# Four of eight weight splits of a pair of heads placed behind the head's chain, sticks and probabilities

## The chip, the cores and the metric

The kernel runs on one core of a Trainium2 chip. The metric is device time in microseconds of one launch; the median over the runs is compared. The engines are TensorE (PE), VectorE (DVE), ScalarE (ACT), GpSimd (POOL) and SyncE (SP), which issues the loads. Each runs its own instructions in order and waits on semaphores.

## The reference

One layer of an encoder with 544 tokens (512 of a prompt, 32 of running streams with 256 cached frames), width 1024, in float32. The part in which the change lies is the combined input projection and the stick-breaking attention of eight heads:

```python
xn = rms_norm(x, g_mix)
h = xn @ w_in              # u | q | k | v | gates
z = jnp.einsum('bqhd,bkhd->bhqk', q, k) * (SB_HEAD_DIM ** -0.5)
causal = k_pos[None, :] < q_pos[:, None]
log_not = jnp.where(causal, jax.nn.log_sigmoid(-z), 0.0)
suffix = lax.cumsum(log_not, axis=3, reverse=True) - log_not
a = jnp.where(causal, jnp.exp(jax.nn.log_sigmoid(z) + suffix), 0.0)
o = jnp.einsum('bhqk,bkhd->bqhd', a, v)
...
merged = gate_a * (y_pool @ w_pool_up) + gate_b * (y_sb @ w_sb_up)
x = x + merged @ w_out
```

Behind it come an MLP and a gated embedding, which the change doesn't touch.

## The kernel before

Each float32 operand is split into a high part (rounded to the type that TensorE takes) and a low part (the rest), and a product is three matmuls: high by high, low by high, high by low. A weight tile is 128 x 1024, made of eight 128 x 128 blocks, and gives a result of 128 x 544 with 48 matmuls.

The stage runs over four pairs of heads; pairs 1 and 2 are a hardware loop, pairs 0 and 3 are written out. A pair has eight weight tiles: 0 to 3 are q, k, v and the pooling input u, 4 to 7 are gates. TensorE's order in pairs 1 and 2 is: tiles 0 and 1, `sums` of head 1 of the pair before, tile 2, its `outputs`, `scores` of head 0, tile 3, `v_rows`, tiles 4 and 5, `sums(0)`, tile 6, `outputs(0)`, `scores(1)`, tile 7. In pair 0 tiles 0 to 3 come ahead of the scores.

**Splits.** `split(t)` stands on two engines. ACT waits until the tile has been loaded to `raw` and a slot of the ring of four split tiles is free, and writes the high part (L853); DVE waits for ACT and writes the low part, raw less high (L1820). The loads (L651, on SP's queue) go to a ring of two buffers: the load of tile t waits until DVE has split tile t - 2, since both share a buffer. Splits run three tiles ahead (`AHEAD`): `split(AHEAD + j)` of pair i is for the tile 3 + j of the pair, so j = 2 and 3 are its tiles 5 and 6, and j = 6 and 7 are tiles 1 and 2 of the next pair. Counted on from the pair's own tiles these are called tiles 9 and 10 below, and the one from j = 5 is tile 8.

**The head's chain.** After `scores`, ACT takes Abs, Exp and Ln of 128 x 1280 (`chain`, L929 to L933); DVE makes the stick, max(z, 0) plus that (`stick`, L1906); GpSimd masks four diagonal blocks (L767); ACT copies the high part (`stick_hi`, L938); DVE adds later blocks (`stick_later`, L1913 to L1916), whose high part ACT takes (L940); DVE takes both low parts (`stick_lo`, L1921 and L1923). TensorE's `sums` need them. Then ACT takes the exponential (`prob`, L946), GpSimd masks it, ACT writes its high part (`prob_hi`, L951), DVE its low part (`prob_lo`, L1927), and `outputs` (L1428, L1430) multiply by V. The parts of stick and of probabilities lie at the same place in `b_hi` and `b_lo`; stick and probabilities share `work`.

**GpSimd** does, beside the masks, the window sums of the pooling mixer (L747), its means (L757 to L760), and issues copies and accumulating copies of weights in HBM (L782, L789) after each head's probabilities, for a later stage. These share the DMA engines with the loads.

The order of each engine is that of the code, written by hand; no scheduler moves anything. What the change moves stands in `pair` of ACT and `pair` of DVE.

Of the kernel before, what the change touches and what calls it, by code (L numbers as in the profile page):

```python
# [32 lines left out]
S1_PER = 8  # L33
# [13 lines left out]
AHEAD = W_RING - 1  # L47
# [250 lines left out]
def hybrid_step_kernel(nc, w_tiles, x_t, p_t, ck_t, cv, state_t, w_grp, vecs,  # L298
# [5 lines left out]
    with ctx:  # L304
# [118 lines left out]
        def rows_of(hh):  # L423
            return slice(DH * hh, DH * hh + DH)
# [416 lines left out]
        def _(act):  # L841
            act.dma_start(vec[:, :], vecs).then_inc(vec_in, 16)

            def split(t, i=0, per=0, left=None):
                if left is None:
                    left = results_by(t - W_RING)

                s = t % W_RING

                act.wait_ge(raw_in[t % RAW_RING], 16 * (t // RAW_RING + t % RAW_RING) + i * (16 * per // RAW_RING))  # L850
                if left is not None:
                    act.wait_ge(full, left + i * per)
                act.activation(w_hi[:, s, :, :].rearrange("p k c -> p (k c)"), raw[:, t % RAW_RING, :],  # L853
                               ACT.Copy).then_inc(whi_done, 1)
# [93 lines left out]
            def prob_hi(hh, i):  # L948
                g = 2 * i + hh
                act.wait_ge(pm_done, g * QB + QB)  # L950
                act.activation(b_hi[:, SOF:SOF + Z_COLS], work[:, :], ACT.Copy).then_inc(phi_done, 1)  # L951
# [16 lines left out]
            def pair(i):  # L968
                first = isinstance(i, int) and i == 0
                last = isinstance(i, int) and i == PAIRS - 1  # L970
                if not first:
                    split(AHEAD + 0, i, S1_PER, 0)
                act.wait_ge(taken, 1 + i * S1_PER)
                for hh in range(2):
                    r = rows_of(hh)
                    act.activation(b_hi[r, QOF + hh * SEQ:QOF + (hh + 1) * SEQ], ev[r, 0, 0:SEQ], ACT.Copy)\
                       .then_inc(qkhi_done, 1)
                if not first:
                    split(AHEAD + 1, i, S1_PER, 1)
                act.wait_ge(taken, 2 + i * S1_PER)  # L980
                for hh in range(2):
                    r = rows_of(hh)
                    act.activation(b_lo[r, KOF + hh * SEQ:KOF + (hh + 1) * SEQ], ev[r, 1, 0:SEQ], ACT.Copy)\
                       .then_inc(qkhi_done, 1)
                act.dma_start(k_t[i, :, :], ev[:, 1, 0:TOK]).then_inc(kv_out[0], 16)
                if first:
                    split(AHEAD + 1)
                if not first:
                    prob(1, i - 1)
                split(AHEAD + 2, i, S1_PER, 2)  # L990
                if not first:
                    prob_hi(1, i - 1)
                chain(0, i)
                split(AHEAD + 3, i, S1_PER, 3)
                stick_hi(0, i)
                act.wait_ge(taken, 3 + i * S1_PER)
                act.dma_start(v_t[i, :, :], ev[:, 2, 0:TOK]).then_inc(kv_out[1], 16)
                act.wait_ge(vt_done, i + 1)
                act.activation(v_parts[:, :, V_HI, :], o_heads, ACT.Copy).then_inc(vhi_done, 1)
                split(AHEAD + 4, i, S1_PER, 4)  # L1000
                if last:

                    tables(SIGMOID)
                    for m in range(KT):
                        sigmoid(m)
                    tables(LOG_EXP)
                    mean_hi(0)
                    mean_hi(1)
                split(AHEAD + 5, i, S1_PER, 5)
                prob(0, i)  # L1010
                split(AHEAD + 6, i, S1_PER, 6)
                prob_hi(0, i)
                if last:
                    group_hi(0)
                    group_hi(1)

                    act.wait_ge(z_done, HEADS)
                    mean_hi(2)
                    mean_hi(3)
                chain(1, i)  # L1020
                split(AHEAD + 7, i, S1_PER, 7)
                if last:
                    group_hi(2)
                    group_hi(3)
                stick_hi(1, i)

            pair(0)
            with act.Fori(1, PAIRS - 1) as i:
# [778 lines left out]
        def _(dve):  # L1807
# [189 lines left out]
            def pair(i):  # L1997
                first = isinstance(i, int) and i == 0
                last = isinstance(i, int) and i == PAIRS - 1
                q, k, v = (ev[:, n, 0:TOK] for n in range(3))  # L2000
                if not first:
                    split(AHEAD + 0, i, S1_PER)

                dve.wait_ge(full, 1 + i * S1_PER)
                dve.scalar_tensor_tensor(out=halves(q), in0=pair_result(0, i), scalar=DH ** -0.5, in1=halves(rn[:, :]),
                                         op0=ALU.mult, op1=ALU.mult).then_inc(taken, 1)
                if first:
                    normed(1, k, i, S1_PER, pair_result(1, i)).then_inc(taken, 1)
                    normed(2, v, i, S1_PER, pair_result(2, i)).then_inc(taken, 1)
                    dve.wait_ge(taken, 3)  # L2010
                if first:
                    q_parts(i)
                    k_parts(i)
                    pool_input(i)
                    split(AHEAD + 1)
                    running_q(i)
                    dve.tensor_copy(kst[:, i, :], k[:, SEQ:TOK])
                    dve.tensor_copy(vst[:, i, :], v[:, SEQ:TOK])
                    split(AHEAD + 2)
                else:  # L2020
                    running_q(i)
                    q_parts(i)
                    split(AHEAD + 1, i, S1_PER)
                    dve.wait_ge(kv_out[0], 16 * i)
                    normed(1, k, i, S1_PER, pair_result(1, i)).then_inc(taken, 1)
                    dve.wait_ge(taken, 2 + i * S1_PER)
                    dve.tensor_copy(kst[:, i, :], k[:, SEQ:TOK])
                    k_parts(i)
                    split(AHEAD + 2, i, S1_PER)
                    prob_lo(1, i - 1)  # L2030
                    dve.wait_ge(kv_out[1], 16 * i)
                    normed(2, v, i, S1_PER, pair_result(2, i)).then_inc(taken, 1)
                    dve.wait_ge(taken, 3 + i * S1_PER)
                    dve.tensor_copy(vst[:, i, :], v[:, SEQ:TOK])
                if not first:
                    head_out(1, i - 1)
                    stick(0, i)
                    split(AHEAD + 3, i, S1_PER)
                    stick_later(0, i)

                if not first:
                    pool_input(i)
                if first:
                    stick(0, i)
                    split(AHEAD + 3)
                    stick_later(0, i)
                stick_lo(0, i)
                dve.wait_ge(vhi_done, i + 1)
                dve.tensor_tensor(v_parts[:, :, V_LO, :], o_heads, v_parts[:, :, V_HI, :], ALU.subtract)\
                   .then_inc(vlo_done, 1)  # L2050
                split(AHEAD + 4, i, S1_PER)
                gate(0, i)
                split(AHEAD + 5, i, S1_PER)
                if last:

                    dve.wait_ge(mean_done, GROUPS)
                gate(1, i)
                split(AHEAD + 6, i, S1_PER)
                if last:
                    mean_lo(0)  # L2060
                    mean_lo(1)
                prob_lo(0, i)
                gate(2, i)
                if last:
                    group_lo(0)
                head_out(0, i)
                if last:
                    group_lo(1)
                    mean_lo(2)
                    mean_lo(3)  # L2070
                    gate(3, i)
                else:
                    split(AHEAD + 7, i, S1_PER)
                stick(1, i)
                if last:
                    group_lo(2)
                    group_lo(3)
                    stick_later(1, i)
                    split(AHEAD + 7, i, S1_PER)
                    stick_lo(1, i)  # L2080
                    for s in kv_out:
                        dve.wait_ge(s, 16 * PAIRS)
                else:
                    gate(3, i)
                    stick_later(1, i)
                    stick_lo(1, i)

            pair(0)
            with dve.Fori(1, PAIRS - 1) as i:
# [472 lines left out]
```

## Time and profile before

| | us |
|---|---|
| runs (three), median | 772.29 (772.29 to 773.46) |
| profiled execution, its own time | 773.24 |
| its span from first to last instruction | 771.5 |
| TensorE busy | 754.4 (98%) |
| DVE busy | 556.8 (72%) |
| ACT busy | 421.9 (55%) |
| GpSimd busy | 147.6 (19%) |
| the pairs of heads | about 34 to 245 of the span |

The mean granted clock of TensorE is 0.995. The busy shares are over the whole program; within the pairs the engines' order and the idle times before each instruction, with what ended them, are in the timelines. A row of a timeline gives the start, the duration, the engine and line, the operation, the tiles written and read, and in brackets the idle time before it and who ended it.

### The profile page before, as it was taken

The page shows a single profiled execution, that of the slowest core. Times are in us where ns is not written, and L with a number is a line of the kernel's source. Part 1 is how long each engine was busy: PE and PEld are TensorE (multiplying, and loading weights), DVE is VectorE, ACT ScalarE, POOL GpSimd, SP SyncE. Part 2 cuts the span into 40 slices and gives each one's busy share as a digit, 9 for nine tenths or more (in the row PEclk, how much of TensorE's full clock was granted, in tenths as well). Part 3 has the DMA queues.
Part 4 walks back from the last instruction along what each step waited for, and adds up shares of the span by engine and source line. Part 5 has one row for each costly group of instructions (what it writes and reads, how often), then busy time and mean ns, then how long its engine had stood idle before and what let it go on. Part 6 is the DMA issues. An engine that isn't in the chain of part 4 may idle for free.

```text
span 771.5 us, 14459 instructions
## 1 busy us (share of the span) xinstructions
PE 754.4 (98%) x5902; PEld 745.6 (97%) x5902; DVE 556.8 (72%) x705; ACT 421.9 (55%) x524; POOL 147.6 (19%) x259
## 2 busy tenths in 40 slices
PE   8999999999999999999999999999999999999994
PEld 8999999999999999999999999999999999999993
DVE  6776556566567527499999669965998567677986
ACT  7545535435485442377674357634763356556575
POOL 1051342453471332001111112111101000000001
PEclk9999999999999999999999999999999999999997
DMA  7254848769769899936797999999887857342503
GB/s 241 91 190 133 233 149 221 228 195 260 221 173 263 264 246 300 256 112 216 215 342 202 370 251 340 250 322 318 236 268 210 281 165 222 107 115 74 198 1 116
DMA packets 49516, 165.78 MB, mean 215 GB/s; under 512 B 6320, under 2 KB 8368, under 8 KB 49456
## 3 DMA queue, kind: packets, MB, share of 16 engines
q0 software_dynamic: 18688, 67.18, 35.2%
q1 hardware_dynamic: 28512, 94.16, 34.9%
q10 hardware_dynamic: 2256, 3.60, 1.3%
q8 instruction: 43, 0.70, 0.3%
q14 instruction: 17, 0.14, 0.1%
HBM read 160.39 MB, written 71.63 MB: 301 GB/s over the span
## 4 chain that ended last, share of the span: by engine, by line
PE 90%; DVE 5%; ACT 3%; issue 1%; DMA 1%; SPq 0%; POOL 0%; POOLq 0%; DVEq 0%
PE psum L1654 23%; PE psum L1705 16%; PE psum L1353 15%; PE psum L1359 14%; PE psum L1356 14%; PE psum L1402 1%; PE psum L1430 1%; DMA raw<-w_tiles 1%; PE psum L1428 1%; PE psum L1390 1%; PE psum L1389 1%; ACT xt L1273 1%; PE psum L1409 1%; PE psum L1414 1%; ACT L887 0%
## 5 line engine op out<-in xcount | busy, mean ns | idle before, releaser
L861 ACT ACTIVATE w_hi<-raw_more 128x1024 fp32r<-128x1024 f32 x83 | 87.7, 1056 | 72.2 <-PE psum L1705 43.3
L1353 PE MATMUL psum<-a_hi,w_hi 128*128 128x272 f32 x576 | 120.5, 290 | 1.4 <-DVE w_lo L1870 1.0
L1828 DVE TENSOR_TENSOR w_lo<-raw_more,w_hi 128x1024 fp32r<-128x1024 f32 x83 | 101.1, 1222 | 25.9 <-ACT w_hi L861 25.5
L1359 PE MATMUL psum<-a_hi,w_lo 128*128 128x272 f32 x576 | 119.2, 288 | 0.0
L1356 PE MATMUL psum<-a_lo,w_hi 128*128 128x272 f32 x576 | 118.8, 288 | 0.0
L1654 PE MATMUL psum<-u_hi,w_hi 128*128 128x272 f32 x560 | 116.3, 289 | 1.5 <-ACT h_of L1105 1.0
L1654 PE MATMUL psum<-u_hi,w_lo 128*128 128x272 f32 x560 | 115.7, 288 | 0.0
L1654 PE MATMUL psum<-u_lo,w_hi 128*128 128x272 f32 x560 | 115.5, 287 | 0.0
L1353 PEld LDWEIGHTS psum<-a_hi,w_hi 128*128 128x128 f32 x576 | 90.3, 188 | 2.0 <-DVE w_lo L1870 1.2
L1356 PEld LDWEIGHTS psum<-a_lo,w_hi 128*128 128x128 f32 x576 | 90.5, 189 | 0.0
L1654 PEld LDWEIGHTS psum<-u_hi,w_hi 128*128 128x128 f32 x560 | 87.9, 188 | 2.4 <-issue 1.9
L1359 PEld LDWEIGHTS psum<-a_hi,w_lo 128*128 128x128 f32 x576 | 89.9, 189 | 0.0
L1654 PEld LDWEIGHTS psum<-u_lo,w_hi 128*128 128x128 f32 x560 | 88.4, 189 | 0.0
L1654 PEld LDWEIGHTS psum<-u_hi,w_lo 128*128 128x128 f32 x560 | 87.4, 188 | 0.0
L1820 DVE TENSOR_TENSOR w_lo<-raw,w_hi 128x1024 fp32r<-128x1024 f32 x41 | 51.2, 1248 | 43.3 <-ACT w_hi L853 43.1
L1828 DVE TENSOR_TENSOR w_lo<-raw,w_hi 128x1024 fp32r<-128x1024 f32 x44 | 53.6, 1222 | 20.6 <-ACT w_hi L861 12.3
L789 POOL DMA_DIRECT2D sums_t<-sums_t x32 | 27.5, 1011 | 192.2 <-PE psum L1654 101.7
L1356 PE MATMUL psum<-b_lo,w_hi 128*128 128x272 f32 x304 | 62.8, 288 | 0.0
L782 POOL DMA_DIRECT2D sums_t<-w_tiles x64 | 33.6, 536 | 150.9 <-DMA sums_t<-w_tiles 51.2
L861 ACT ACTIVATE w_hi<-raw 128x1024 fp32r<-128x1024 f32 x39 | 41.2, 1056 | 36.0 <-PE psum L1705 21.7
L853 ACT ACTIVATE w_hi<-raw 128x1024 fp32r<-128x1024 f32 x46 | 48.1, 1050 | 22.0 <-DMA raw<-w_tiles 13.2
L1353 PE MATMUL psum<-b_hi,w_hi 128*128 128x272 f32 x288 | 60.0, 289 | 0.0
(287 smaller groups left out, 1562.7 us busy)
## 6 DMA issues: line engine op xcount, KB each, us to landing
sums_t<-w_tiles POOLq DMA_DIRECT2D x96, 512.0 KB, 8.1
raw<-w_tiles SPq DMA_DIRECT2D x63, 512.0 KB, 4.4
raw_more<-sums_t SPq DMA_DIRECT2D x42, 512.0 KB, 6.7
raw_more<-w_tiles SPq DMA_DIRECT2D x41, 512.0 KB, 5.1
sums_t<-sums_t POOLq DMA_DIRECT2D x32, 512.0 KB, 10.9
raw<-sums_t SPq DMA_DIRECT2D x22, 512.0 KB, 5.0
xt<-x_t SPq DMA_DIRECT2D x8, 272.0 KB, 5.8
y_t<-xt SPq DMA_DIRECT2D x16, 136.0 KB, 1.9
```

The costliest lines, as they stand in the source:

```text
L782: pool.dma_start(sum_tile(i, what), sum_tile(i, of)).then_inc(sums_in, 16)
L789: pool.dma_start(sum_tile(i, what), sum_tile(i, of), accum_op=ALU.add).then_inc(sums_in, 16)
L853: act.activation(w_hi[:, s, :, :].rearrange("p k c -> p (k c)"), raw[:, t % RAW_RING, :], ACT.Copy).then_inc(whi_done, 1)
L861: act.activation(w_hi[:, t % W_RING, :, :].rearrange("p k c -> p (k c)"), src, ACT.Copy)\
L1273: act.activation(x, x, ACT.Copy, scale=g_fin[:, m:m + 1]).then_inc(xg_last, 1)
L1353: pe.matmul(base[:, h, :], w_hi[:, s, wk, :], at(hi, k, h * HALF, (h + 1) * HALF), start=(opens and q == 0), stop=False, skip_group_check= ...
L1356: pe.matmul(base[:, h, :], w_hi[:, s, wk, :], at(lo, k, h * HALF, (h + 1) * HALF), start=False, stop=False, skip_group_check=True)
L1359: mm = pe.matmul(base[:, h, :], w_lo[:, s, wk, :], at(hi, k, h * HALF, (h + 1) * HALF), start=False, stop=(closes and q == len(ks) - 1), s ...
L1654: mm = pe.matmul(out[:, two, :], w_part[:, t % W_RING, 2 * k + two, :], u_part[:, op, k, :], start=(OPENS[s] and k == 0 and w_part is w_hi ...
L1705: mm = pe.matmul(out[:, two, :], w_part[:, t % W_RING, 2 * k + two, :], h_part[:, i * HALF:(i + 1) * HALF], start=(OPENS[s] and k == 0 and ...
L1820: dve.tensor_tensor(w_lo[:, s, :, :].rearrange("p k c -> p (k c)"), raw[:, t % RAW_RING, :], w_hi[:, s, :, :].rearrange("p k c -> p (k c)" ...
L1828: dve.tensor_tensor(w_lo[:, t % W_RING, :, :].rearrange("p k c -> p (k c)"), src, w_hi[:, t % W_RING, :, :].rearrange("p k c -> p (k c)"), ...
```

## The change

In each pair four splits are placed later, on both engines. On ACT: tile 5 behind `prob_hi` of the head before (it stood between `prob` and `prob_hi`), tile 6 behind `stick_hi(0)` (between `chain` and `stick_hi`), tile 9 behind `prob_hi(0)`, tile 10 behind `stick_hi(1)`. On DVE: tile 5 behind `prob_lo`, tile 6 from between `stick` and `stick_later` to behind `stick_lo`, tile 9 behind `prob_lo(0)`, tile 10 from ahead of `stick(1)` to behind `stick_lo(1)`. In pair 0 there is no head before, so tile 5 stays. TensorE's, GpSimd's and SP's programs are the same.

```diff
--- ACT, pair(i)
-                split(AHEAD + 2, i, S1_PER, 2)
+
                 if not first:
                     prob_hi(1, i - 1)
+                split(AHEAD + 2, i, S1_PER, 2)
                 chain(0, i)
+                stick_hi(0, i)
                 split(AHEAD + 3, i, S1_PER, 3)
-                stick_hi(0, i)
...
                 prob(0, i)
+                prob_hi(0, i)
                 split(AHEAD + 6, i, S1_PER, 6)
-                prob_hi(0, i)
...
                 chain(1, i)
-                split(AHEAD + 7, i, S1_PER, 7)
                 if last:
                     group_hi(2)
                     group_hi(3)
                 stick_hi(1, i)
+                split(AHEAD + 7, i, S1_PER, 7)
--- DVE, pair(i)
                     k_parts(i)
+                    prob_lo(1, i - 1)
                     split(AHEAD + 2, i, S1_PER)
-                    prob_lo(1, i - 1)
...
                     stick(0, i)
-                    split(AHEAD + 3, i, S1_PER)
                     stick_later(0, i)
...
                 if first:
                     stick(0, i)
-                    split(AHEAD + 3)
                     stick_later(0, i)
                 stick_lo(0, i)
+                split(AHEAD + 3, i, S1_PER)
...
-                split(AHEAD + 6, i, S1_PER)
                 if last:
                     mean_lo(0)
                     mean_lo(1)
                 prob_lo(0, i)
+                split(AHEAD + 6, i, S1_PER)
...
-                else:
-                    split(AHEAD + 7, i, S1_PER)
                 stick(1, i)
                 if last:
...
                     stick_later(1, i)
+                    stick_lo(1, i)
                     split(AHEAD + 7, i, S1_PER)
-                    stick_lo(1, i)
...
                     stick_later(1, i)
                     stick_lo(1, i)
+                    split(AHEAD + 7, i, S1_PER)
```

ACT in pair 0, from the end of head 0's chain (`work`) over the stick's high parts (`b_hi`, `later_hi`), V's (`b_hi` from `psum`) and the exponential, before:

```order
L933 ACTIVATE work<-work 128x1280
L853 ACTIVATE w_hi<-raw 128x1024
L938 ACTIVATE b_hi<-work 128x1280
L940 ACTIVATE later_hi<-later 128x384
L997 DMA v_t<-ev 128x544
L999 ACTIVATE b_hi<-psum 128x4x2x64
L853 ACTIVATE w_hi<-raw 128x1024 x2
L946 ACTIVATE work<-psum 128x1280
L853 ACTIVATE w_hi<-raw 128x1024
L951 ACTIVATE b_hi<-work 128x1280
```

The same place after (lines further down count one more):

```order
L933 ACTIVATE work<-work 128x1280
L938 ACTIVATE b_hi<-work 128x1280
L940 ACTIVATE later_hi<-later 128x384
L853 ACTIVATE w_hi<-raw 128x1024
L998 DMA v_t<-ev 128x544
L1000 ACTIVATE b_hi<-psum 128x4x2x64
L853 ACTIVATE w_hi<-raw 128x1024 x2
L946 ACTIVATE work<-psum 128x1280
L951 ACTIVATE b_hi<-work 128x1280
L853 ACTIVATE w_hi<-raw 128x1024
```

The first L853 (tile 6) moved past the stick's two high parts, the last (tile 9) past the probabilities'; the pair between them (tiles 7 and 8) stays in its place.

DVE at the same place, from the stick (`work`) to the low part of V (L2049), before:

```order
L1906 SCALAR_TENSOR_TENSOR work<-psum,work 128x1280
L1820 TENSOR_TENSOR w_lo<-raw,w_hi 128x1024
L1913 TENSOR_TENSOR later<-work 128x128
L1914 TENSOR_TENSOR later<-work 128x128
L1916 TENSOR_TENSOR later<-work,later 128x128
L1921 TENSOR_TENSOR b_lo<-work,b_hi 128x1280
L1923 TENSOR_TENSOR later_lo<-later,later_hi 128x384
L2049 TENSOR_TENSOR b_hi<-psum,b_hi 128x4x128
```

and after:

```order
L1907 SCALAR_TENSOR_TENSOR work<-psum,work 128x1280
L1914 TENSOR_TENSOR later<-work 128x128
L1915 TENSOR_TENSOR later<-work 128x128
L1917 TENSOR_TENSOR later<-work,later 128x128
L1922 TENSOR_TENSOR b_lo<-work,b_hi 128x1280
L1924 TENSOR_TENSOR later_lo<-later,later_hi 128x384
L1821 TENSOR_TENSOR w_lo<-raw,w_hi 128x1024
L2049 TENSOR_TENSOR b_hi<-psum,b_hi 128x4x128
```

The split of tile 6 moved from ahead of the three later sums to behind the two low parts, ahead of V's low part (L2049).

## Rows read from the trace of the kernel before

**Rows 1.** The page's first part: busy us, share of the span, instructions.

```profile
PE 754.4 (98%) x5902; PEld 745.6 (97%) x5902; DVE 556.8 (72%) x705; ACT 421.9 (55%) x524; POOL 147.6 (19%) x259
```

**Rows 2.** Busy time by stretch: length, engines, clock, DMA share, GB/s.

```profile
34.00:94.40 60.40, 59.93 (x464) 58.96 (x463) 41.02 (x55) 31.77 (x31) 18.32 (x33) 1.00 0.56 178
94.40:152.80 58.40, 58.40 (x458) 57.88 (x457) 35.33 (x48) 26.91 (x27) 21.90 (x39) 1.00 0.69 199
...
128.00:132.00 4.00, 4.00 (x35) 4.00 (x33) 3.85 (x6) 1.57 (x3) 0.00 (x0) 1.00 0.48 149
```

**Rows 3.** TensorE's waits, 34 to 262 us: total, times, longest.

```profile
PE psum L1353 <- issue: 1.1, 1, 1.1
```

**Rows 4.** Timeline of TensorE: start, us, instruction, idle time before and releaser.

```profile
50.55 0.46 PE L1353 MATMUL psum<-a_hi,w_hi 128*128 128x272 f32 x2
...
56.63 0.50 PE L1428 MATMUL psum<-b_hi 128*128 128x512 f32 x1
...
115.18 0.39 PE L1428 MATMUL psum<-b_hi 128*128 128x512 f32 x1
```

**Rows 5.** Timeline of DVE, pairs 0 to 2.

```profile
38.95 1.49 DVE L1906 SCALAR_TENSOR_TENSOR work<-psum,work 128x1280 f32<-128x1280 f32 x1 [1.25 <-ACT work L933]
40.74 1.23 DVE L1820 TENSOR_TENSOR w_lo<-raw,w_hi 128x1024 fp32r<-128x1024 f32 x1 [0.30 <-ACT w_hi L853]
...
44.02 1.26 DVE L1916 TENSOR_TENSOR later<-work,later 128x128 f32<-128x128 f32 x1
45.20 1.48 DVE L1921 TENSOR_TENSOR b_lo<-work,b_hi 128x1280 fp32r<-128x1280 f32 x1
46.60 0.55 DVE L1923 TENSOR_TENSOR later_lo<-later,later_hi 128x384 fp32r<-128x384 f32 x1
...
54.67 1.91 DVE L1927 TENSOR_TENSOR b_lo<-work,b_hi 128x1280 fp32r<-128x1280 f32 x1
...
100.95 1.55 DVE L1820 TENSOR_TENSOR w_lo<-raw,w_hi 128x1024 fp32r<-128x1024 f32 x1
...
113.06 1.49 DVE L1927 TENSOR_TENSOR b_lo<-work,b_hi 128x1280 fp32r<-128x1280 f32 x1 [0.27 <-ACT b_hi L951]
...
122.70 1.23 DVE L1820 TENSOR_TENSOR w_lo<-raw,w_hi 128x1024 fp32r<-128x1024 f32 x1 [4.59 <-ACT w_hi L853]
...
135.96 0.72 DVE L1865 TENSOR_TENSOR ev<-psum,rn 128x544 f32<-128x544 f32 x1 [0.19 <-PE psum L1359]
```

**Rows 6.** Timeline of ACT, pairs 0 to 2.

```profile
46.22 2.00 ACT L853 ACTIVATE w_hi<-raw 128x1024 fp32r<-128x1024 f32 x2
50.75 1.24 ACT L946 ACTIVATE work<-psum 128x1280 f32<-128x1280 f32 x1 [2.53 <-PE psum L1402]
...
53.37 1.26 ACT L951 ACTIVATE b_hi<-work 128x1280 fp32r<-128x1280 f32 x1
...
111.75 1.27 ACT L951 ACTIVATE b_hi<-work 128x1280 fp32r<-128x1280 f32 x1 [0.26 <-POOL work L767]
...
132.84 1.06 ACT L853 ACTIVATE w_hi<-raw 128x1024 fp32r<-128x1024 f32 x1
...
138.31 1.24 ACT L946 ACTIVATE work<-psum 128x1280 f32<-128x1280 f32 x1 [0.31 <-PE psum L1402]
```

**Rows 7.** Timeline of GpSimd (POOL), pair 0.

```profile
40.51 2.11 POOL L767 TENSOR_SCALAR_AFFINE_SELECT work<-work 128x128 f32<-128x128 f32 x4 [36.44 <-DVE work L1906]
...
52.12 1.04 POOL L767 TENSOR_SCALAR_AFFINE_SELECT work<-work 128x128 f32<-128x128 f32 x4 [7.00 <-ACT work L946]
...
55.23 2.84 POOL L757 TENSOR_SCALAR gates<-gates 128x557 f32<-128x557 f32 x1
```

**Rows 8.** Loads issued near 42, 113 and 124: KB, us to landing.

```profile
raw<-w_tiles SPq DMA_DIRECT2D x1, 512.0 KB, 3.5
...
raw<-w_tiles SPq DMA_DIRECT2D x1, 512.0 KB, 9.7
...
raw<-w_tiles SPq DMA_DIRECT2D x1, 512.0 KB, 7.4
```

## The prediction

> **What bounds the kernel now.** I read the page's busy shares first: TensorE is busy for 754.4 of the 771.5 us [rows 1]. Then the busy time by stretch: the whole change lies in the four pairs of heads, from 34 to 245 us. In the pairs' first stretch TensorE is busy for 59.93 of 60.40 us and in the next for 58.40 of 58.40, at the full clock (1.00, the 2.4 GHz level) [rows 2]. The reader should see that there is nothing to win there but 0.47 us of idle time, which lies before tile 4 of pair 0, ahead of every edit, and 1.1 us at the end of the last pair, where TensorE begins the pooled tiles [rows 3]. So the ceiling of any gain is about 1.6 us, and the question is whether the change puts a new wait on TensorE. Its program is the same before and after; what changes is when the operands arrive. For that I read the timelines of DVE, ACT and GpSimd around pair 0 and pair 1 and looked for the smallest margin between an operand's end and the matmul that needs it. It is in pair 0: the low half of head 0's probabilities ends at 54.67 + 1.91 = 56.58 [rows 5] and the product with V starts at 56.63 [rows 4]. In pair 1 the same step ends at 113.06 + 1.49 = 114.55 and is needed at 115.18: 0.63 us of margin [rows 4, 5]. Pair 0 is tight because its tile 3 is done before the scores, so one tile of 6.1 us fewer (50.55 to 56.63 is tile 6) stands between scores and sums.
>
> **The splits of tiles 5 and 9 (behind the high half of the probabilities; numbers by the pair's own count).** In pair 1 ACT's high half starts at 111.75 after 0.26 us of idle time that the masks on GpSimd ended [rows 6]: the split ran inside the wait for the masks, so moving it frees nothing there. DVE's low half started 0.27 us after its split [same pair, rows 5], again on ACT's end. The split itself comes 1.3 us (ACT) and about 2.9 us (DVE: 1.49 for the low half that is now first, 1.3 for the later start) later, and with it the next load of its buffer. Cost 0: behind either place TensorE still has two tiles of 6.1 us or more to do before it needs them. Pair 0 has no such step for tile 5.
>
> **The split of tile 6 (behind stick).** In pairs 1 to 3 the gain is in GpSimd: four masks took 2.11 us with a split on DVE beside them (40.51, split at 40.74) and 1.04 without (52.12) [rows 5, 7]. The stick chain comes 1 us earlier, and that is off the path. The Trainium skill says why (SBUF — State Buffer, Who interferes with whom): a VectorE instruction with two SBUF inputs contends with a GpSimd instruction that reads SBUF. These rows agree.
>
> The split then ends, in pair 1, about where the next one does now (100.95 + 1.55 = 102.5 [rows 5]) or sooner, and tile 6 starts near 109.1 (115.18 less a tile): no wait. In pair 0, step by step:
> - Stick ends at 38.95 + 1.49 = 40.44, the masks at 40.51 + 1.04 = 41.55 instead of 42.62: 1.07 earlier.
> - The three later sums end at 45.28 now (44.02 + 1.26), so at 44.2. From there to the end of the two low halves it is 1.95 us now (45.20 to 46.60 + 0.55): 46.15.
> - ACT does the split after the sums' high half: 44.25 + 0.5 + 1.06 = 45.8. DVE does it after the low halves: 46.15 + 1.2 = 47.35, instead of 40.74 + 1.23 = 41.97. Tile 6 starts at 50.55: 3.2 us of margin, no wait of TensorE.
> - But the raw ring has two buffers, so tile 8's load waits for this split. It was issued near 42 and landed after 3.5 us [rows 8], ahead of its place on ACT (the second of the two splits from 46.22, near 47.2 [rows 6]). Now it is issued at 47.4 and lands at 50.9. ACT stands in that wait with the probabilities behind it: split 50.95 to 52.0, exponential from 51.9 instead of 50.75: 1.15 late.
> - Exponential 1.24, masks 1.04, high half: it can start at 54.25 instead of 53.37 (0.88 late, since the split of tile 9 no longer stands before it). High half 1.28, so the low half starts on DVE at 55.55 and takes 1.49 (row of pair 1) to 1.91 (row of this place): 57.05 to 57.45.
> - TensorE, which came for it at 56.63, waits 0.4 to 0.8 us. I take 0.7, nearer to the row of this place.
>
> The same page says that whichever of the two starts first holds the pair of ports for its whole instruction, and the other blocks. The low half would start at 55.55, ahead of GpSimd's scaling (55.23 now, and about 1 us later then), and so run in 1.49: 0.4 us of wait, 772.7 in all. The row of now speaks against it: 1.91 at 54.67, though it began 0.56 us before the scaling [rows 5, 7].
>
> Bounds of this term: if DVE's later sums get ahead of GpSimd's window sums (the last of them, 128 x 128, takes 1.26 us here, as long as a split of 128 x 1024 [rows 5], so it is held up), tile 8's load comes 1 us sooner and the wait is 0; if the load took 9.7 us, the worst of the pairs' loads [rows 8], it is 7 us. That worst row was issued among the copies of sums, with the DMA engines full; 47 us is ahead of the first copies, which follow the masks of 52.12, so I take 3.5.
>
> **The split of tile 10 (behind stick of head 1).** DVE's stick no longer waits for the split, so head 1's chain comes about 2 us sooner; TensorE has tile 0 and tile 1 of the next pair before it needs it. The split's end moves by 4.9 us in pair 1, from 122.70 + 1.23 = 123.9 [rows 5] to about 128.8 (after ACT's two steps of stick and DVE's two low halves), and with it the load of the tile that ACT splits at 132.84 [rows 6]. That load took 7.4 us when issued at 124 [rows 8], among copies; at 128 to 132 the DMA engines are 0.48 busy [rows 2], so I take 4 us: landed at 132.8, no cost. The last pair's 1.1 us hangs on gate and group work that isn't moved: unchanged.
>
> **Sum.** 0 + 0.7 + 0 on the profiled execution's 773.24 gives 773.9. That execution is 0.95 above the median of the runs shown, 772.29; against that median it is 773.0, which I forecast.
>
> **Rivals.**
> 1. No wait at all (the lower bound above): 772.3. For it: the 1.07 us that the masks give back, and each of the chain's estimates is only 0.3 us wide. Against: the zero margin at 56.58.
> 2. Faster: the earlier chains close some idle time of TensorE. At most 1.6 us of it is in the stretch, and I find no edit that reaches either piece; 771 at best.
> 3. Slower, by one mechanism: the load behind the split of tile 10 stays among the copies. If it takes 7.4 us again, it lands at 136.3; ACT 1.06 and DVE 1.23 make 138.6, and the new keys (behind that split on DVE, due at 135.96 [rows 5]) follow at 138.7, 2.7 late; ACT converts them ahead of head 1's probabilities, whose exponential starts at 138.31 [rows 6] after 0.3 us of idle time. Less that and about 0.6 us of margin at the product with V, TensorE waits some 1.8 us, in pairs 1 to 2 and 2 to 3 each: 773.0 + 3.6 = 776.6, or 774.8 if only one pair. It decides from a landing time of about 5.5 us. For it: in this stretch loads take 7.4 to 9.7. Against: the copies are nearly done by 128.
> 4. The change does what it says but the load of tile 8 is slower still, by 1 us: 774.0; it belongs to the forecast's own range.
>
> **How the numbers follow.** Forecast (a wait of 0.3 to 1.5 us in pair 0): 0.48. No wait: 0.29. Slower by late loads: 0.19. Faster: 0.04. A measurement of this kernel can tell about 0.2%, 1.5 us, from no change. Forecast and rival 1 lie within it, less a few hundredths where small waits add up: same 0.76, slower 0.21, faster 0.03. The likeliest case alone spans 772.5 to 773.9; the range takes in no wait, with the runs' own spread below it, and one late load: 771.9 to 775.0.
>
> **What would show it.** In the profile after: masks of head 0 near 1.04 us in every pair; tile 8's split on ACT waiting for a DMA until about 51 us; the exponential of pair 0 near 51.9; a wait of 0.4 to 0.8 us before the product with V near 57, named to DVE's b_lo; and no wait of TensorE in pairs 1 and 2. I am wrong if that wait is missing, if TensorE waits for w_lo anywhere in the pairs, or if ACT waits for raw in pairs 2 and 3 so long that the probabilities slip.

## The result, and the profile after

The changed kernel takes 773.52 us (median of 14 runs, 772.83 to 775.28), the kernel before 772.64 in the runs beside it (14 runs, 772.15 to 773.54). The ratio is 1.0015, with a 95% interval of 1.0008 to 1.0022: about 0.15% slower, below the 0.2% that the prediction named as the least that can be told, though the interval leaves 1 out. The forecast was 773.0, the range 771.9 to 775.0. The profiled execution took 773.29 us, its span 771.5 us at a clock of 0.995, as before.

The sum line of the page hardly moves (answers to [rows 1]):

```profile
PE 754.7 (98%) x5902; PEld 745.6 (97%) x5902; DVE 559.5 (73%) x705; ACT 421.7 (55%) x524; POOL 145.2 (19%) x259
```

The busy time by stretch (length, then busy time and instructions of PE, PEld, DVE, ACT, POOL, then clock, DMA share, GB/s; answers to [rows 2]) says in which pair something happened:

```profile
34.00:94.40 60.40, 59.32 (x460) 58.22 (x459) 39.94 (x54) 30.60 (x30) 16.45 (x33) 1.00 0.55 172
94.40:152.80 58.40, 58.40 (x458) 57.88 (x458) 36.12 (x47) 26.92 (x27) 20.98 (x39) 1.00 0.73 198
152.80:211.30 58.50, 58.48 (x457) 57.74 (x456) 36.37 (x47) 26.80 (x27) 23.67 (x40) 1.00 0.84 222
```

TensorE has 0.61 us less in pair 0's stretch than before; the next two are as full as they were, but for 0.02 us in the last (58.50 of 58.50 before). To place it, I lined up the 5902 matmuls of the two traces one by one and looked where the difference of their start times steps. It is -0.44 us before the first edit (the start of a run varies: the kernel before, profiled again, began the pairs 0.15 earlier), and then steps four times: +0.75 at pair 0's product with V, +0.29 at the product of pair 2's head 1 (203 us), +0.21 in the last pair (234 us), and -0.77 at 362 us, far behind the change. At the end it is +0.05: the earlier start hides most of the cost in these two traces.

**Pair 0.** Timeline of TensorE after (start, us, instruction, idle time before and releaser; answers to [rows 4]):

```profile
56.94 0.50 PE L1429 MATMUL psum<-b_hi 128*128 128x512 f32 x1 [0.60 <-DVE b_lo L1928]
...
115.49 0.39 PE L1429 MATMUL psum<-b_hi 128*128 128x512 f32 x1
```

The wait is there in pair 0 and not in pair 1. Its origin is on ACT (answers to [rows 6]; L853 is a split, L946 the exponential, L951 the probabilities' high half):

```profile
44.24 1.04 ACT L853 ACTIVATE w_hi<-raw 128x1024 fp32r<-128x1024 f32 x1
...
45.67 1.05 ACT L853 ACTIVATE w_hi<-raw 128x1024 fp32r<-128x1024 f32 x1
50.61 1.06 ACT L853 ACTIVATE w_hi<-raw 128x1024 fp32r<-128x1024 f32 x1 [3.89 <-DMA raw<-w_tiles]
51.58 1.22 ACT L946 ACTIVATE work<-psum 128x1280 f32<-128x1280 f32 x1
54.00 1.27 ACT L951 ACTIVATE b_hi<-work 128x1280 fp32r<-128x1280 f32 x1 [1.21 <-POOL work L767]
```

The row at 50.61 is the one to see: tile 8's split stands 3.89 us for its load, and the exponential follows it without a gap. That load went out once DVE had done tile 6's split (45.57 + 1.21, below) and landed after 3.6 us:

```profile
raw<-w_tiles SPq DMA_DIRECT2D x1, 512.0 KB, 3.6
```

DVE in the same stretch (answers to [rows 5]), then GpSimd (answers to [rows 7]):

```profile
42.51 1.26 DVE L1917 TENSOR_TENSOR later<-work,later 128x128 f32<-128x128 f32 x1
...
45.57 1.21 DVE L1821 TENSOR_TENSOR w_lo<-raw,w_hi 128x1024 fp32r<-128x1024 f32 x1
...
55.31 1.58 DVE L1928 TENSOR_TENSOR b_lo<-work,b_hi 128x1280 fp32r<-128x1280 f32 x1 [1.74 <-ACT b_hi L951]
```

```profile
40.07 1.04 POOL L767 TENSOR_SCALAR_AFFINE_SELECT work<-work 128x128 f32<-128x128 f32 x4 [36.00 <-DVE work L1907]
...
56.04 2.34 POOL L757 TENSOR_SCALAR gates<-gates 128x557 f32<-128x557 f32 x1
```

The masks take 1.04 us instead of 2.11, and the later sums end 1.5 us earlier (0.44 of it the start); the exponential is still 0.83 later (1.27 with the start taken off), because it now queues behind a load.

**Between pairs 2 and 3.** The two weight loads issued between 186.5 and 189 us took 5.9 us, and one of them is the tile that ACT splits at 193.59. The loads, and the timelines of ACT, DVE and TensorE after:

```profile
raw<-w_tiles SPq DMA_DIRECT2D x2, 512.0 KB, 5.9
```

```profile
193.59 1.06 ACT L853 ACTIVATE w_hi<-raw 128x1024 fp32r<-128x1024 f32 x1 [2.85 <-DMA raw<-w_tiles]
...
197.88 1.24 ACT L946 ACTIVATE work<-psum 128x1280 f32<-128x1280 f32 x1
...
201.56 1.49 DVE L1928 TENSOR_TENSOR b_lo<-work,b_hi 128x1280 fp32r<-128x1280 f32 x1 [2.85 <-ACT b_hi L951]
...
203.11 0.50 PE L1429 MATMUL psum<-b_hi 128*128 128x512 f32 x1
```

The same place before: no wait for the load, the exponential 1.1 us earlier (0.8 with pair 0's lag taken off). The first matmul's row is 0.50 us long after and 0.40 before: the lost time stands inside a busy share, and only the start times show it.

```profile
191.28 1.06 ACT L853 ACTIVATE w_hi<-raw 128x1024 fp32r<-128x1024 f32 x1
...
196.75 1.24 ACT L946 ACTIVATE work<-psum 128x1280 f32<-128x1280 f32 x1 [0.24 <-PE psum L1402]
...
202.61 0.40 PE L1428 MATMUL psum<-b_hi 128*128 128x512 f32 x1
```

**The last pair.** TensorE's step is at 234.79, at the first matmul behind the product with V. It starts 0.05 us behind the end of the DVE row that takes a gate's result out of `psum`, where TensorE writes its results (`gates<-psum`, 234.02 + 0.72), and tile 9's split now stands between the low half and that row. After:

```profile
231.48 1.49 DVE L1928 TENSOR_TENSOR b_lo<-work,b_hi 128x1280 fp32r<-128x1280 f32 x1 [1.30 <-ACT b_hi L951]
232.89 1.22 DVE L1821 TENSOR_TENSOR w_lo<-raw,w_hi 128x1024 fp32r<-128x1024 f32 x1
234.02 0.72 DVE L1942 TENSOR_TENSOR gates<-psum,rn 128x544 f32<-128x544 f32 x1
...
234.79 0.39 PE L1335 MATMUL psum<-b_lo,b_hi 128*128 128x272 f32 x1
```

Before, that row ended at 233.07, 0.96 us ahead of its matmul. In the six traces with tile 9 late in the last pair (this one, numbers 1, 3, 6, 11 and 12) the matmul starts 0.05 to 0.06 us behind the row's end; in the other eight the row ends 0.96 to 0.97 us ahead of it. DVE couldn't start the low half sooner to make up for it: with the split out of the way, its mean_lo comes a split earlier and runs beside the masks of the probabilities, which take twice as long (after, then before):

```profile
228.10 2.04 POOL L767 TENSOR_SCALAR_AFFINE_SELECT work<-work 128x128 f32<-128x128 f32 x4 [2.48 <-ACT work L946]
...
228.49 0.70 DVE L1988 TENSOR_TENSOR mean_lo<-upad,mean_hi 128x512 fp32r<-128x512 f32 x1
...
230.17 1.27 ACT L951 ACTIVATE b_hi<-work 128x1280 fp32r<-128x1280 f32 x1 [2.14 <-POOL work L767]
```

```profile
227.49 1.03 POOL L767 TENSOR_SCALAR_AFFINE_SELECT work<-work 128x128 f32<-128x128 f32 x4 [2.42 <-ACT work L946]
...
228.56 1.28 ACT L951 ACTIVATE b_hi<-work 128x1280 fp32r<-128x1280 f32 x1 [0.19 <-POOL work L767]
```

So the low half starts at 231.48, against 230.95 before, which is about TensorE's own lag of 0.61, though the split no longer stands ahead of it. Which of the two, the split's place or the longer masks, would be enough by itself was not tried.

**At 362 us** TensorE meets ACT's evictions (L1105, one line lower after). Before, then after:

```profile
361.44 0.60 ACT L1105 ACTIVATE h_of<-psum 128x544 f32<-128x544 f32 x1
...
362.15 0.48 PE L1654 MATMUL psum<-u_hi,w_hi 128*128 128x272 f32 x2 [0.53 <-issue]
```

```profile
361.36 0.60 ACT L1106 ACTIVATE h_of<-psum 128x544 f32<-128x544 f32 x1
...
362.29 0.42 PE L1655 MATMUL psum<-u_hi,w_hi 128*128 128x272 f32 x2
```

The profile names no releaser for the 0.53 us. But in all fourteen traces of this study that matmul starts, within 0.02 us, at the later of two times: 0.12 us behind the matmul before it, or 0.10 us behind the end of that eviction (before: 361.33 + 0.12 against 362.05 + 0.10; after: 362.17 + 0.12 against 361.96 + 0.10). ACT's chain was 0.09 us earlier after, TensorE 0.84 later; so 0.77 us of what TensorE lost upstream (0.70 at this matmul, the rest at the next) was lost where it would have waited anyway. The longest wait of ACT's chain ahead of it is for a weight load among GpSimd's copies (its split at 325.94 waited 7.15 us before, the one at 329.42 4.53 us after). What sets these landings in one execution was not tried.

### The profile page after: what moved, and what is told of

It reads as the page before. It is cut to its first block, busy times and chain, and to the rows that moved or that the text cites. A ratio compares the mean times of both kernels' runs of the same rounds, so it can differ in the third digit from the quotient of the medians.

```text
span 771.5 us, 14459 instructions
## 1 busy us (share of the span) xinstructions
PE 754.7 (98%) x5902; PEld 745.6 (97%) x5902; DVE 559.5 (73%) x705; ACT 421.7 (55%) x524; POOL 145.2 (19%) x259
## 4 chain that ended last, share of the span: by engine, by line
PE 85%; issue 6%; DVE 4%; ACT 3%; POOL 1%; DMA 0%; POOLq 0%; SPq 0%; DVEq 0%
PE psum L1655 23%; PE psum L1706 16%; PE psum L1354 13%; PE psum L1360 13%; PE psum L1357 13%; PE psum L1403 1%; PE psum L1429 1%; PE psum L1431 1%; PE psum L1391 1%; PE psum L1390 1%; ACT xt L1274 1%; ACT L887 0%; DMA raw<-w_tiles 0%; PE psum L1410 0%; DVE w_lo L1829 0%
## 5 line engine op out<-in xcount | busy, mean ns | idle before, releaser
L1821 DVE TENSOR_TENSOR w_lo<-raw,w_hi 128x1024 fp32r<-128x1024 f32 x41 | 54.5, 1338 | 20.5 <-ACT w_hi L853 20.4
L1829 DVE TENSOR_TENSOR w_lo<-raw,w_hi 128x1024 fp32r<-128x1024 f32 x44 | 53.6, 1222 | 19.4 <-ACT w_hi L861 12.3
L853 ACT ACTIVATE w_hi<-raw 128x1024 fp32r<-128x1024 f32 x46 | 47.9, 1049 | 33.9 <-DMA raw<-w_tiles 27.1
```

The source lines that it names most:

```text
L1821: dve.tensor_tensor(w_lo[:, s, :, :].rearrange("p k c -> p (k c)"), raw[:, t % RAW_RING, :], w_hi[:, s, :, :].rearrange("p k c -> p (k c)" ...
L1829: dve.tensor_tensor(w_lo[:, t % W_RING, :, :].rearrange("p k c -> p (k c)"), src, w_hi[:, t % W_RING, :, :].rearrange("p k c -> p (k c)"), ...
```

## The experiments

All ratios are against the kernel before on the same chip in the same job, with 95% intervals. "Step" is a step of the difference of matmul starts against the trace of the kernel before, counted over all the matmuls over which it grows.

**1. Pair 0's tile 6 back in its place** (all else as changed):

```diff
+                if first:
+                    split(AHEAD + 3, i, S1_PER, 3)
                 stick_hi(0, i)
-                split(AHEAD + 3, i, S1_PER, 3)
+                if not first:
+                    split(AHEAD + 3, i, S1_PER, 3)
```

(the same on DVE).

> The changed kernel with tile 6's split in pair 0 alone back in its old place on both engines. Theory (the late split holds up the load of tile 8, and ACT stands in that wait with the exponential behind it): TensorE's 0.60 us of idle time before pair 0's product with V is gone, its program runs 0.75 us earlier from there on, and the two smaller steps in pair 3 (0.29 and 0.16 us) stay; time about 0.4 to 0.5 us over the kernel before, ratio near 1.0006. Rival (DVE and GpSimd get in each other's way at the low half of the probabilities, whatever the load does): at least 0.4 us of that wait stays. Second rival (the loss is in pairs 1 to 3): time as the changed kernel, ratio near 1.0015.

Measured: 772.63 against 772.71, ratio 1.0001 [0.9992, 1.0010]. No wait and a step of -0.13 at pair 0's product (its first matmul takes 0.40 us, that of the kernel before 0.50 [rows 4], so that kernel loses a little there too), +0.42 at 203, +0.21 at 234, -0.57 at 362.

```profile
49.95 1.24 ACT L946 ACTIVATE work<-psum 128x1280 f32<-128x1280 f32 x1 [2.62 <-PE psum L1406]
...
55.82 0.40 PE L1432 MATMUL psum<-b_hi 128*128 128x512 f32 x1
```

With one split in one pair put back, no difference is left that can be measured.

**2. Only pair 0's tile 6 late** (the kernel before with that one edit):

```diff
-                split(AHEAD + 3, i, S1_PER, 3)
+                if not first:
+                    split(AHEAD + 3, i, S1_PER, 3)
                 stick_hi(0, i)
+                if first:
+                    split(AHEAD + 3, i, S1_PER, 3)
```

> The kernel before with tile 6's split of pair 0 alone placed late on both engines. Theory: the wait of 0.6 us before pair 0's product with V is there, and no other new one; TensorE is 0.75 us later from there; ratio near 1.0008 to 1.0010. Second rival (the loss is in pairs 1 to 3): no wait, ratio 1.0000.

Measured: 773.40 against 772.71, ratio 1.0010 [1.0001, 1.0019]. One step of +1.13 at pair 0's product, none else in the pairs, -0.46 at 362: +0.66 from start to end, and +0.69 by the medians.

```profile
51.00 1.06 ACT L853 ACTIVATE w_hi<-raw 128x1024 fp32r<-128x1024 f32 x1 [3.90 <-DMA raw<-w_tiles]
51.97 1.22 ACT L946 ACTIVATE work<-psum 128x1280 f32<-128x1280 f32 x1
...
57.72 0.50 PE L1431 MATMUL psum<-b_hi 128*128 128x512 f32 x1 [1.00 <-DVE b_lo L1930]
```

The edit makes the cost by itself. The step is larger than in the changed kernel, mainly because the low half takes 1.92 us, not 1.58; tile 9's split still stands ahead of it here (see the last section).

**3. Keep tile 6 late, take tile 8's split from ahead of the exponential** (the changed kernel; in pair 0 tile 8's split behind both halves; ACT's side):

```diff
-                split(AHEAD + 5, i, S1_PER, 5)
+                if not first:
+                    split(AHEAD + 5, i, S1_PER, 5)
                 prob(0, i)
                 prob_hi(0, i)
+                if first:
+                    split(AHEAD + 5, i, S1_PER, 5)
```

> The changed kernel with tile 8's split in pair 0 also moved, behind the high and low half of the probabilities; tile 6's split stays late, so the load of tile 8 lands as late as in the changed kernel (near 50.6). Theory (the late load costs time only because ACT waits for it ahead of the exponential): the exponential starts when the sums end, about 1.2 us sooner than in the changed kernel, and the 0.60 us wait before the product with V is gone; the steps of pair 3 stay; ratio near 1.0006. Rival (contention on DVE and GpSimd): the wait stays at 0.4 us or more.

Measured: 772.42 against 772.71, ratio 0.9994 [0.9985, 1.0003]. Pair 0 has no wait, and the -0.13 of number 1; the load is as late, but nothing that matters stands behind it:

```profile
50.66 1.24 ACT L946 ACTIVATE work<-psum 128x1280 f32<-128x1280 f32 x1 [3.60 <-PE psum L1406]
...
56.52 0.40 PE L1432 MATMUL psum<-b_hi 128*128 128x512 f32 x1
```

So it is the place of the wait in ACT's order, not the late split or the late load, that costs.

**4. The kernel before again**, as a control.

> The kernel before, unchanged, as a control. Every theory: ratio 1.0000 within the interval. Its trace tells whether two differences between the traces of before and after belong to the change: TensorE's start, 0.44 us earlier after, which lies ahead of every edit, and an idle time of 0.53 us at 362 us that stood in before alone. If either differs between two runs of this same kernel, it belongs to the run and not to the change.

Measured: 772.91, ratio 1.0000 [0.9991, 1.0009]. Steps: -0.15 at the start, +0.06 at pair 0's product and no other in the pairs, -0.14 at 362, where the wait is 0.39 us.

**5. Only tile 10 late; 6. only tiles 5 and 9 late** (the kernel before with these edits of the change alone; ACT's side of 5, then of 6):

```diff
-                split(AHEAD + 7, i, S1_PER, 7)
                 if last:
                     group_hi(2)
                     group_hi(3)
                 stick_hi(1, i)
+                split(AHEAD + 7, i, S1_PER, 7)
```

```diff
-                split(AHEAD + 2, i, S1_PER, 2)
                 if not first:
                     prob_hi(1, i - 1)
+                split(AHEAD + 2, i, S1_PER, 2)
...
-                split(AHEAD + 6, i, S1_PER, 6)
                 prob_hi(0, i)
+                split(AHEAD + 6, i, S1_PER, 6)
```

> The kernel before with only the split of tile 10 (all pairs) placed late, behind stick of head 1. Theory A (the step of 0.29 us at 203 us in the changed kernel is this split's load: issued near 188 among the copies of sums, it lands too late for the next pair, and ACT's conversion of k and the exponential behind it slip): an idle time of 0.2 to 0.5 us of TensorE before pair 3's first product with V, ACT waiting for raw near 191 to 193, and nothing new in pair 0; ratio 1.0000 to 1.0006. Rival (the step comes from the other three splits, or from the 0.75 us by which pair 0 is late): no wait there.

> The kernel before with only the splits of tiles 5 and 9 placed late, behind the high and low halves of the probabilities. Theory B (the step of 0.16 us at 234 us is GpSimd's masks in the last pair: without the split DVE reaches the low halves of the means while the masks run, both read SBUF, and the masks take 2 us instead of 1): masks near 227.5 take about 2.0 us, the high half starts about 1 us later, TensorE is 0.1 to 0.2 us late from its product with V in the last pair on; no other new wait; ratio 1.0000 to 1.0004. Rival (these two moves cost nothing): masks at 1.03, no step.

Measured: 772.78, ratio 1.0001 [0.9992, 1.0010], and 772.39, ratio 0.9994 [0.9985, 1.0003]. With tile 10 late TensorE has no step in the pairs: ACT waits 1.94 us for the load before the split at 191.68 (landing 5.0 us), and the product takes it without delay. With tiles 5 and 9 late there is +0.21 at 234, with masks of 2 us as in the changed kernel, and -0.14 at pair 0's product, where tile 9's split no longer stands ahead of the low half; nothing else in the pairs.

**7. An order meant to be better: in the last pair group_lo(2) ahead of stick(1), and tile 10's split behind the halves of stick** (the kernel before; DVE's side):

```diff
+                    group_lo(2)
...
                 stick(1, i)
...
-                    group_lo(2)
                     group_lo(3)
                     stick_later(1, i)
-                    split(AHEAD + 7, i, S1_PER)
                     stick_lo(1, i)
+                    split(AHEAD + 7, i, S1_PER)
```

**8. The same group_lo in the changed kernel**, with the edit of 3, and the last pair's tile 9 in its old place (ACT's side):

```diff
+                if last:
+                    split(AHEAD + 6, i, S1_PER, 6)
                 prob_hi(0, i)
-                split(AHEAD + 6, i, S1_PER, 6)
...
+                if not last:
+                    split(AHEAD + 6, i, S1_PER, 6)
```

> The kernel before, in the last pair only: DVE takes the low half of pooled group 2 ahead of head 1's stick, and the split of tile 10 stands behind that stick's halves on both engines. Every theory: the 1.1 us of idle time before the first pooled tile shrinks by 0.5 to 0.7 us, since DVE's stick (1.48 us) no longer stands ahead of what frees the result slot. Theory C (the stage that follows, the output projection, is paced by ACT, DVE and the landing of loads and not by TensorE, so that it swallows a few tenths of lead or lag): most of it is lost again at 362 us, where TensorE waits longer; ratio 0.9997 to 1.0000. Rival (TensorE paces all of it): the gain stays, ratio 0.9992.

> The changed kernel with what the runs so far point to: in pair 0 tile 8's split also behind the probabilities (no wait before the product with V), in the last pair the split of tile 9 back in its old place (masks at 1.03 us), and DVE's low half of pooled group 2 ahead of head 1's stick. Theory: no new wait of TensorE against the kernel before in the pairs, 0.5 us less idle time before the pooled tiles; time between 771.6 and 772.6, ratio 0.9985 to 1.0000; under theory C nearer to the upper end. Rival (the late loads of the tile 10 splits cost in any case): 0.3 us of wait in pair 3 stays and the ratio is 1.0000 or more.

Both missed. Measured: 774.34, ratio 1.0016 [1.0002, 1.0030], and 773.10, ratio 1.0011 [0.9995, 1.0027]. Each trace has a wait that no other has, at the first product with the past keys, for the load of the past values: 0.95 us in 7, 1.94 in 8. TensorE in 7, the landing of the two past loads in 7, and their landing in the kernel before:

```profile
262.40 1.77 PE L1547 MATMUL psum<-qbd,ckt 128*128 128x64 f32 x14 [0.95 <-DMA cvn<-cv]
```

```profile
ckt<-ck_t ACTq DMA_DIRECT2D x1, 512.0 KB, 6.0
cvn<-cv ACTq DMA_DIRECT2D x1, 512.0 KB, 8.3
```

```profile
ckt<-ck_t ACTq DMA_DIRECT2D x1, 512.0 KB, 3.6
cvn<-cv ACTq DMA_DIRECT2D x1, 512.0 KB, 4.6
```

The weight loads that wait for the late split go out at 251.8 us in 7 instead of 247.7, close ahead of the past loads (253.4 and 254.1).

**9. group_lo(2) ahead of stick(1) alone**, tile 10's split where it was:

```diff
+                    group_lo(2)
...
                 stick(1, i)
...
-                    group_lo(2)
                     group_lo(3)
```

> The kernel before with one edit in the last pair: group_lo(2) ahead of stick(1) on VectorE; the last split of that pair (tile 10) where it was. Theory: what made the earlier run with both edits slower is not this order but the late split: its tile's buffer came free late, the 512 KB weight loads went out at 251.8 instead of 247.7 us, and the load of the past values behind them landed 8.3 us after its issue instead of 4.6, 0.95 us after TensorE wanted it. Without the late split these loads go out at about 248.5 to 249.5, the past values land within 5 us, TensorE does not wait at its first product with the past keys, and the ratio is 0.9993 to 1.0005. Rival: the later stick (244.6 against 243.0) is the cost by itself, and the ratio stays at 1.001 to 1.0025 with no wait on a load.

Measured: 772.37 against 772.43, ratio 0.9997 [0.9988, 1.0006]; the past values land after 6.5 us, and TensorE does not wait. The later stick by itself costs nothing that was measured. Nor does the late split by itself make TensorE wait there: in the changed kernel those weight loads go out at 251.0, the past values' load goes out at 255.4, 1.3 us later than in 7, and lands after 6.7 us, in time. Number 9's trace has a step of +0.69 at pair 0's product, where nothing was edited (see the last section). So the size of that step in one trace doesn't settle a cost; the medians of numbers 1, 2 and 3 do.

**10. The changed kernel mended**: the edit of 3, and in the last pair the splits of tiles 9 (as in 8) and 10 (as below) in their old places. **11. Only the last pair's tile 10 back** (ACT's side). **12. The changed kernel again.**

```diff
                 if last:
+                    split(AHEAD + 7, i, S1_PER, 7)
                     group_hi(2)
                     group_hi(3)
                 stick_hi(1, i)
-                split(AHEAD + 7, i, S1_PER, 7)
+                if not last:
+                    split(AHEAD + 7, i, S1_PER, 7)
```

> The changed kernel with three edits: tile 8's split of pair 0 behind the halves of the probabilities, and in the last pair the splits of tiles 9 and 10 where the kernel before has them. Theory: each of the three took a wait or a lost margin away that a trace showed (0.75 us in pair 0, 0.15 at 234, the margin of the past values' load at 262), so nothing of the change's cost is left: 772.0 to 772.6, ratio 0.9990 to 1.0000. Rival: the orders are worth nothing either way and the ratio is 1.0000 +- 0.0005.

> The changed kernel with one edit: the last pair's split of tile 10 where the kernel before has it. Theory: in the changed kernel's trace the past values land 262.1 us and TensorE wants them at 262.25, a margin of 0.16 us (2.3 us before), so that in some executions it waits there and the times have a tail (5 of 14 above 774.0, none before). With the split back the loads go out about 3 us earlier, the past values land within 5 us of their issue, the tail is gone and the median falls by 0.2 to 0.5 us, to 773.0 to 773.3, ratio 1.0004 to 1.0009. Rival: the tail is pair 0's or pair 3's wait, varying, and both tail and ratio (1.0010 to 1.0015) stay as they were.

> The changed kernel, unchanged, as a control for the run with its last split put back. Theory and rival alike: ratio 1.0010 to 1.0020, with a few times above 774.0. By the theory its trace shows a wait on the past values' load at the first product with the past keys if the profiled execution falls in the tail, and a margin below 0.5 us if not; by the rival the margin has nothing to do with the time.

Measured, against 772.43: 10 took 772.24, ratio 0.9995 [0.9986, 1.0004]; 11 took 773.91, ratio 1.0015 [1.0006, 1.0024]; 12 took 773.63, ratio 1.0016 [1.0007, 1.0025]. Number 10 has the -0.13 at pair 0's product and no other step in the pairs. Number 11 refutes its theory: the margin at the past values is wide again (they land after 5.0 us), and time and spread stay. The small margin at 262 us in the changed kernel costs nothing that was measured; pair 0's wait does. Number 10 takes the cost away, but its interval holds 1: nothing here is shown to beat the kernel before.

## Why the prediction was right, and where its terms were off

- **Tile 6 in pair 0: right, term by term.** Named: masks 1.04, DVE's split from 46.15, the load out at 47.4 and down at 50.9, ACT's split 50.95, the exponential 51.9, the low half at 55.55, a wait of 0.4 to 0.8. The trace, which runs 0.44 us early: 1.04, 45.57, near 46.9 and 50.6, 50.61, 51.58, 55.31, a wait of 0.60 and a step of 0.75 against 0.7. Numbers 1, 2 and 3 show the chain: without the edit no cost, with it alone the cost, and with the waiting split moved away none.
- **The low half between 1.49 and 1.91: 1.58.** The rule of the Trainium skill (SBUF — State Buffer, SBUF: two separate sides) that the first to start holds the ports would give 1.49; it fits here better than the row I leaned on. It does not hold in number 9 (last section).
- **Tile 10 at 0: mis-sized by 0.29 us.** Between pairs 1 and 2 the load out at 129 landed after 3.6 us, as said. Between pairs 2 and 3 it took 5.9, past the 5.5 from which rival 3 decides, and the product was 0.29 late. Every trace with tile 10 late between these pairs falls in line: where ACT waits for this load for 1.94 to 2.55 us, and it lands after at most 5.6 (numbers 5, 8, 3 and 10), the step is 0; at 2.63 us of waiting it is 0.06 (11), at 2.85 it is 0.29, at 2.94 it is 0.37 (12), at 3.00 it is 0.42 (1). Rival 3 was the right mechanism at the right threshold, but 1.8 us a pair was for 7.4 us of landing. By one of its own signs the prediction failed here: it called itself wrong if ACT waited for `raw` in pairs 2 and 3 so long that the probabilities slip, and they slipped, the exponential by 0.8 us and the product by 0.29.
- **Tiles 5 and 9 at 0: missed by 0.21 us.** I counted when the moved splits' own tiles are needed, and not what stands behind a split in its new place, nor what moves up into the old one. In the last pair DVE's eviction of a gate's result now stands behind tile 9's split, and mean_lo moved up beside the masks; number 6 has the same step with these two edits alone, and numbers 8 and 10, with tile 9 back there, have none.
- **Given back at 362: not foreseen, 0.77 us.** I took TensorE's lost time as lost for good. Behind the pairs ACT's chain sets the time in the kernel before: 0.53 us of wait in its trace, 0.39 in number 4.
- **The level.** I counted from 772.29, a median of three runs; the fourteen gave 772.64. With that base the same sum gives 773.3. In the traces the change costs 0.75 + 0.29 + 0.21 - 0.77 = 0.48 us, in the timed runs 0.9 and (number 12) 1.2. That medians and single traces differ by this much stays open: the steps at pair 0's product, at 203 and at 362 us vary between executions, and one trace shows one of them. That the time came out near the forecast is in part luck: what was missed at tiles 5, 9 and 10 (0.50 us) and what was given back at 362 have opposite signs.

## What to carry to other kernels

A step that is moved back also moves the load that waits for its buffer, and the engine that splits the loaded tile stands in that wait with everything queued behind it: price a late load at the first instruction on the path that is queued behind its consumer, and move the consumer rather than the load. Look also at what stands behind the step in its new place, at what moves up into the place that was left, and at the next point where another chain sets the time, since a lag is paid there only as far as it is longer than the wait.

## What the runs showed of the hardware

Who slows whom between DVE and GpSimd turned on a few tenths of a microsecond. Pair 0's low half starts before GpSimd's scaling in every trace. With a lead of 0.72 to 0.74 us it takes 1.58 to 1.59 (scaling 2.34 to 2.36, eight traces); with 0.50 to 0.67 us it takes 1.91 to 1.92 (scaling 2.75 to 2.91, four traces); with 0.35 us, as here in number 9, it takes 2.38 and the scaling only 1.67, and TensorE waits in a pair 0 that was not edited:

```profile
54.52 2.38 DVE L1927 TENSOR_TENSOR b_lo<-work,b_hi 128x1280 fp32r<-128x1280 f32 x1
...
56.96 0.50 PE L1428 MATMUL psum<-b_hi 128*128 128x512 f32 x1 [0.54 <-DVE b_lo L1927]
```

```profile
54.87 1.67 POOL L757 TENSOR_SCALAR gates<-gates 128x557 f32<-128x557 f32 x1
```

So the later of the two was not the one held up; number 7 shows the same (2.39 and 1.67). In the twelve traces with a lead of 0.50 us or more the scaling ends 1.49 to 1.50 us behind the end of the low half; in 7 and 9 the low half ends 0.36 us behind the scaling. The eight traces with 1.58 to 1.59 are those in which tile 9's split stands behind the low half; in the other six DVE comes straight from that split. What decides between the cases was not tried.

In number 8 TensorE stood idle for 1.94 us in its wait for the past values, to 262.7 us; in the 1.1 us from 264.90 the granted clock was 0.50, the 1.2 GHz level:

```profile
261.00:262.70 1.70, 0.00 (x0) 0.00 (x0) 1.63 (x3) 0.00 (x0) 0.00 (x0) 1.00 1.02 410
262.70:264.90 2.20, 2.19 (x16) 2.15 (x16) 0.92 (x1) 0.00 (x0) 0.00 (x0) 0.85 1.08 359
264.90:266.00 1.10, 1.10 (x10) 0.85 (x9) 0.00 (x0) 0.00 (x0) 0.00 (x0) 0.50 1.02 264
```

From the end of the wait to 267.5 us its matmuls fell a further 1.5 us behind. In number 7, after 0.95 us of waiting, the clock stayed at 1.00.
